# A trunk kernel's sample tile: V sums and gate products in two 64-column halves side by side, and identity products in TensorE's idle time

## What is computed

```python
h = h + mixer(rmsnorm(h, norm_mix))           # GLA and gated-delta heads, w_in, w_out
a = rmsnorm(h, norm_ffn)
q = a @ w_pq                                   # 8 heads, 2 halves of 128
idx, gate = top16_of_products(q, sub_keys)     # 16 experts of 16384 per token and head
hid = gelu(einsum('td,thkd->thk', a, u_tab[idx]))
h = h + einsum('thk,thkd->td', gate * hid, v_tab[idx])
gate = sigmoid(rmsnorm(h, norm_ple) @ w_ple_gate + b_ple_gate)
h = h + gate * (p @ w_ple_proj)
# after the last layer: y = rmsnorm(h, norm_final)
```

## Time and profile before

| | |
|---|---|
| median of three runs | 2375.65 us |
| profiled execution | 2375.78 us, span 2374.3 us |
| TensorE products | busy 1774.1 us, 75% |
| TensorE weight loads | busy 976.9 us, 41% |
| VectorE | busy 1452.3 us, 61% |
| ScalarE | busy 690.6 us, 29% |
| GpSimd | busy 1305.5 us, 55% |
| HBM read | 752.7 MB, 321 GB/s over the span |
| TensorE's granted clock, mean of the span | 0.874 of full speed |

### The profile page before, as it was taken

The page is one execution under the profiler, slowest core; times in us unless marked ns, Lnnn a source line. Parts: engine busy times, 40 slices in busy tenths (PEclk is TensorE's granted clock), DMA queues, the critical chain, the costliest instruction groups (busy, mean ns, idle before and its releaser), DMA issues.

```text
span 2374.3 us, 26318 instructions
## 1 busy us (share of the span) xinstructions
PE 1774.1 (75%) x9032; PEld 976.9 (41%) x9032; DVE 1452.3 (61%) x3698; ACT 690.6 (29%) x1641; POOL 1305.5 (55%) x1387
## 2 busy tenths in 40 slices
PE   7999998766566655579889999977655566555897
PEld 5768763322122211135567687533221222112354
DVE  2545556666766766676426446656666777667665
ACT  3323332222223222232333323322221332322232
POOL 2022257667777777767300232566677777776762
PEclk9999998888768778799999999988887777687999
DMA  8320299999999999999663204999999999999994
GB/s 242 107 91 22 84 394 400 406 406 406 409 409 409 409 409 409 409 405 404 232 204 108 81 15 149 393 402 406 406 406 409 409 409 409 409 409 406 407 402 161
DMA packets 268450, 763.26 MB, mean 321 GB/s; under 512 B 27002, under 2 KB 99634, under 8 KB 268312
## 3 DMA queue, kind: packets, MB, share of 16 engines
q0 software_dynamic: 187424, 682.78, 72.8%
q1 hardware_dynamic: 80888, 78.74, 10.4%
HBM read 752.70 MB, written 8.72 MB: 321 GB/s over the span
## 4 chain that ended last, share of the span: by engine, by line
PE 36%; DMA 32%; POOL 14%; DVE 9%; issue 6%; ACT 3%; SPq 0%; DVEq 0%; POOLq 0%; ACTq 0%
PE ps L1922 35%; DMA arena<-in_peer_u_dram,idx_u 32%; POOL arena L776 8%; POOL arena L785 6%; DVE arena L1439 3%; ACT arena L1103 1%; DVE arena L1628 0%; DVE arena L1326 0%; PE ps L1930 0%; DMA h<-in_x_sample_dram 0%; DVE wgt L1447 0%; DVE xn L1831 0%; ACT L853 0%; DVE top L1276 0%; ACT xn L1070 0%
## 5 line engine op out<-in xcount | busy, mean ns | idle before, releaser
L1922 PE MATMUL ps<-arena 64*64 64x512 f32 (+6 forms) x5856 | 1063.1, 668 | 540.9 <-ACT arena L1103 529.0
L1439 DVE CUSTOM_DVE_ANT_0 arena<-arena,ps 128x1024 f32<-128x1024 f32 x640 | 779.9, 1221 | 516.2 <-DMA arena<-in_peer_u_dram,idx_u 492.7
L1922 PEld LDWEIGHTS ps<-arena 64*64 64x64 f32 (+4 forms) x5856 | 444.6, 180 | 1098.9 <-issue 968.7
L785 POOL DMA_INDIRECT arena<-in_peer_v_dram,idx_u x640 | 605.0, 945 | 304.7 <-PE ps L1922 166.7
L776 POOL DMA_INDIRECT arena<-in_peer_u_dram,idx_u x640 | 609.3, 952 | 247.2 <-issue 173.7
L1922 PE MATMUL ps<-aT,wring 128*128 128x320 f32 (+1 forms) x1280 | 368.2, 444 | 2.3 <-ACT aT L1079 2.3
L1096 ACT ACTIVATE gelu<-hid 128x4 f32<-128x4 f32 x160 | 32.9, 206 | 1079.2 <-DVE hid L1439 1079.2
L1922 PEld LDWEIGHTS ps<-aT,wring 128*128 128x128 f32 x1280 | 244.2, 196 | 146.4 <-issue 58.2
L1922 PE MATMUL ps<-wring,aT 128*128 128x256 f32 x960 | 219.2, 383 | 3.1 <-DVE h L1810 1.6
L1922 PEld LDWEIGHTS ps<-wring,aT 128*128 128x128 f32 x960 | 179.1, 190 | 49.0 <-issue 26.9
L1103 ACT ACTIVATE arena<-ident,wgt 128x128 f32<-128x128 f32 x512 | 163.5, 390 | 72.9 <-DVE wgt L1447 72.9
(11 more groups left out here) (338 smaller groups left out, 1343.2 us busy)
## 6 DMA issues: line engine op xcount, KB each, us to landing
wring<-in_w_in_dram SPq DMA_DIRECT2D x28, 1024.0 KB, 5.6
wring<-in_w_peer_q_dram SPq DMA_DIRECT2D x18, 1024.0 KB, 18.3
arena<-in_peer_u_dram,idx_u POOLq DMA_INDIRECT x640, 16.2
arena<-in_peer_v_dram,idx_u POOLq DMA_INDIRECT x640, 15.9
wring<-in_w_out_dram SPq DMA_DIRECT2D x8, 1024.0 KB, 5.1
wring<-in_w_ple_gate_dram SPq DMA_DIRECT2D x8, 1024.0 KB, 16.6
arena<-in_state_gdn_dram POOLq DMA_DIRECT2D x2, 2048.0 KB, 18.9
out_dram<-arena SPq DMA_DIRECT2D x2, 2048.0 KB, 8.7
```

The source lines that it names most:

```text
L785: pool.indirect_dma_start(vrow[:, n % G, :], None, v_l, bass.IndirectOffsetOnAxis(ap=at, axis=0)).then_inc(v_loaded[n % G], 16)
L1439: dve.tensor_tensor_reduce(out=urow[:, n % G, :], in0=urow[:, n % G, :], in1=x_bank, scale=1.0, scalar=0.0, op0=ALU.mult, op1=ALU.add, acc ...
L1922: return pe.matmul(out, lhsT, rhs, start=start, stop=stop, skip_group_check=True)
```

## The change

For tile 2, whose doubled half is given up in most places:

- TensorE's V products: the stationary is 128 x 64 (ScalarE writes 64 columns of diag), bank m of the sum goes to partitions 64m to 64m+63, so the two products of an expert stand on the two column halves of the array. A first pair with the identity puts h itself into the sum. The sum is then copied into h, bank 0 by VectorE (64 rows), bank 1 by ScalarE (copy_half, from the upper partitions to the lower).
- The gates: for each r in 0, 1 the products m = 2r and 2r+1 alternate over k, 64 columns each, into the lower and the upper half. VectorE's work after them goes by r (2 times) and not by m (4 times). project does the same with its outputs; next_scale, square, the transposes and the last scaling work on 64 rows.
- GpSimd copies h's sample rows to the upper partitions at the start of each layer, which the mixer's w_out sum and the experts still need; VectorE and GpSimd wait for it (gvm_ready 1; the old gvm_ready 1 becomes 2).
- v1 of tile 2 is made by two 64-column products side by side, so that it still lies in both halves; aT is copied without its last 64 columns.
- keep_busy(n) issues n products of the identity with reset (320 columns) into bank 7, which nobody reads: 5 before the first layer, 6 before the last quad (with a wait for ple_done 8 ahead), 14 after the gates.

The diff, cut to its core:

```diff
@@ -305,11 +305,13 @@
-            return ps[:, 4 + m if i == 2 else 6 + m % 2, 0:WCOLS]
+            if i == 2:
+                return ps[HALF * (m % 2):HALF * (m % 2) + HALF, 4 + m // 2, 0:WCOLS]
+            return ps[:, 6 + m % 2, 0:WCOLS]
-                return ps[:, 2 + m // 2, WCOLS * (m % 2):WCOLS * (m % 2 + 1)]
+                return ps[HALF * (m % 2):HALF * (m % 2) + HALF, 2 + m // 2, 0:WCOLS]
...
@@ -668,6 +671,8 @@
+                pool.wait_ge(start_norm, 9)
+                pool.tensor_copy(h[HALF:P, 2, :], h[0:HALF, 2, :]).then_inc(gvm_ready, 1)
...
@@ -675,6 +680,7 @@
+                pool.wait_ge(gvm_ready, 1)
...
@@ -827,7 +833,7 @@
-                    act.activation(aT[:, k, :], ps[:, k % 4, 0:TILES * P], ACT.Copy,
+                    act.activation(aT[:, k, 0:NT], ps[:, k % 4, 0:NT], ACT.Copy,
...
@@ -1098,9 +1104,10 @@
+                    cols = P if step < 2 * HP else HALF
-                        act.activation(diag[:, n % G, :], unit[:, :], ACT.Copy,
+                        act.activation(diag[:, n % G, 0:cols], unit[:, 0:cols], ACT.Copy,
...
@@ -1144,9 +1151,18 @@
-                    act.wait_ge(h_added, i + 1 if i < 2 else 4)
-                    act.activation(xn[:, i, :], h[:, i, :], ACT.Square,
-                                   accum_out=ssq[:, i:i + 1]).then_inc(sq_done, 1)
+                    R = ROWS[i]
+                    act.wait_ge(h_added, i + 1)
+                    if i == 2:
+                        act.wait_ge(h_copied, 1)
+                    act.activation(xn[0:R, i, :], h[0:R, i, :], ACT.Square,
+                                   accum_out=ssq[0:R, i:i + 1]).then_inc(sq_done, 1)
+                def copy_half():
+                    act.wait_ge(v_free, G + TOPK * NSTEP)
+                    act.activation(h[0:HALF, 2, BANK:2 * BANK], ps[HALF:P, ACC_BANK[2] + 1, :],
+                                   ACT.Copy).then_inc(h_copied, 1)
...
@@ -1204,16 +1221,16 @@
+                copy_half()
-                for m in range(4):
-                    act.wait_ge(ple_biased, m + 1)
-                    act.activation(sig[:, m % 2, :], sig[:, m % 2, :], ACT.Sigmoid
-                                   ).then_inc(ple_sig, 1)
+                for r in range(2):
+                    act.wait_ge(ple_biased, r + 1)
+                    act.activation(sig[:, r, :], sig[:, r, :], ACT.Sigmoid).then_inc(ple_sig, 1)
-                act.activation(rstd[:, 2:3], ssq[:, 2:3], ACT.Sqrt).then_inc(std_ready, 1)
+                act.activation(rstd[0:HALF, 2:3], ssq[0:HALF, 2:3], ACT.Sqrt).then_inc(std_ready, 1)
...
@@ -1457,14 +1474,16 @@
-                    for b in range(2):
-                        c = slice(BANK * b, BANK * (b + 1))
-                        dve.tensor_tensor(h[:, i, c], h[:, i, c], bank(ACC_BANK[i] + b), ALU.add
-                                          ).then_inc(h_added, 1)
+                    dve.tensor_copy(h[0:HALF, i, 0:BANK], ps[0:HALF, ACC_BANK[i], :]
+                                    ).then_inc(h_added, 1)
-                dve.tensor_scalar(ssq[:, i:i + 1], ssq[:, i:i + 1], 1.0 / D, EPS, ALU.mult,
+                if i == 2:
+                    dve.tensor_scalar(ssq[HALF:P, i:i + 1], ssq[0:HALF, i:i + 1], 1.0 / D, EPS,
+                                      ALU.mult, ALU.add)
+                R = ROWS[i]
+                dve.tensor_scalar(ssq[0:R, i:i + 1], ssq[0:R, i:i + 1], 1.0 / D, EPS, ALU.mult,
...
@@ -1776,6 +1797,7 @@
+                dve.wait_ge(gvm_ready, 1)
...
@@ -1891,21 +1913,32 @@
-                for m in range(4):
-                    c = slice(WCOLS * m, WCOLS * (m + 1))
-                    dve.wait_ge(ple_mm, 9 + m)
-                    dve.scalar_tensor_tensor(sig[:, m % 2, :], gate_of(2, m), rstd[:, 2:3],
-                                             gain_row[:, c], ALU.mult, ALU.add
-                                             ).then_inc(ple_biased, 1)
-                    embed(2, m, own)
-                    dve.wait_ge(ple_done, 9 + m)
+                for r in range(2):
+                    dve.wait_ge(ple_mm, 9 + r)
+                    for g_ in range(2):
+                        rows, m = slice(HALF * g_, HALF * g_ + HALF), 2 * r + g_
+                        ins = dve.scalar_tensor_tensor(
+                            sig[rows, r, :], gate_of(2, m), rstd[rows, 2:3],
+                            gain_row[rows, WCOLS * m:WCOLS * (m + 1)], ALU.mult, ALU.add)
+                    ins.then_inc(ple_biased, 1)
+                    dve.wait_ge(ple_sig, 9 + r)
+                    own.after(dve.tensor_tensor(sig[:, r, :], sig[:, r, :], ps[:, 2 + r, 0:WCOLS],
+                                                ALU.mult))
+                    own.settle()
+                    for g_ in range(2):
+                        there = h[0:HALF, 2, WCOLS * (2 * r + g_):WCOLS * (2 * r + g_ + 1)]
+                        own.after(dve.tensor_tensor(
+                            there, there, sig[HALF * g_:HALF * g_ + HALF, r, :], ALU.add))
+                    own.settle()
+                    c = slice(BANK * r, BANK * (r + 1))
-                        out=xn[:, 2, c], in0=h[:, 2, c], in1=h[:, 2, c], scale=1.0, scalar=0.0,
-                        op0=ALU.mult, op1=ALU.add, accum_out=ssq_part[:, m:m + 1]))
+                        out=xn[0:HALF, 2, c], in0=h[0:HALF, 2, c], in1=h[0:HALF, 2, c], scale=1.0,
+                        scalar=0.0, op0=ALU.mult, op1=ALU.add, accum_out=ssq_part[0:HALF, r:r + 1]))
-                own.after(dve.tensor_reduce(ssq[:, 2:3], ssq_part[:, :], AX, ALU.add))
+                own.after(dve.tensor_tensor(ssq[0:HALF, 2:3], ssq_part[0:HALF, 0:1],
+                                            ssq_part[0:HALF, 1:2], ALU.add))
-                dve.tensor_scalar(ssq[:, 2:3], ssq[:, 2:3], 1.0 / D, EPS, ALU.mult, ALU.add
+                dve.tensor_scalar(ssq[0:HALF, 2:3], ssq[0:HALF, 2:3], 1.0 / D, EPS, ALU.mult, ALU.add
...
@@ -1913,7 +1946,9 @@
-                dve.tensor_tensor(xn[:, i, :], xn[:, i, :], fin_row, ALU.mult).then_inc(xn_ready, 1)
+                R = ROWS[i]
+                dve.tensor_tensor(xn[0:R, i, :], xn[0:R, i, :], fin_row[0:R, :], ALU.mult
+                                  ).then_inc(xn_ready, 1)
...
@@ -1958,7 +1993,13 @@
+            def keep_busy(count):
+                for _ in range(count):
+                    mm(ps[:, 7, 0:NT], ident[:, :], reset[:, :])
+            keep_busy(5)
...
@@ -1999,8 +2040,10 @@
-                            ins = mm(ps[:, b, 0:WCOLS], aT[:, k, P * i:P * (i + 1)],
-                                     wring[:, blk % RING, k, :], k == 0, k == KD - 1)
+                            for t0 in (0, HALF) if i == 2 else (0,):
+                                R = ROWS[i]
+                                ins = mm(ps[t0:t0 + R, b, 0:WCOLS], aT[:, k, COL[i]:COL[i] + R],
+                                         wring[:, blk % RING, k, :], k == 0, k == KD - 1)
...
@@ -2120,7 +2163,7 @@
-                pe.wait_ge(gvm_ready, 1)
+                pe.wait_ge(gvm_ready, 2)
...
@@ -2314,8 +2357,12 @@
-                                ins = mm(bank(ACC_BANK[tile] + m), diag[:, n % G, :],
-                                         vrow[:, n % G, BANK * m:BANK * (m + 1)], opens, False)
+                                there = ps[HALF * m:HALF * m + HALF, ACC_BANK[tile] + m, :]
+                                if opens:
+                                    mm(there, ident[0:HALF, 0:HALF],
+                                       h[0:HALF, 2, BANK * m:BANK * (m + 1)], True, False)
+                                ins = mm(there, diag[:, n % G, 0:HALF],
+                                         vrow[:, n % G, BANK * m:BANK * (m + 1)], False, False)
...
@@ -2462,7 +2509,7 @@
-                        mm(emb_of(i, m), pT[:, k, P * i:P * (i + 1)],
+                        mm(emb_of(i, m), pT[:, k, COL[i]:COL[i] + ROWS[i]],
...
@@ -2491,6 +2538,9 @@
+                    if q4 == NQUAD - 1:
+                        pe.wait_ge(ple_done, 8)
+                        keep_busy(6)
...
@@ -2508,21 +2558,27 @@
-                    pe.wait_ge(h_added, 3 + b)
+                    if b == 0:
+                        pe.wait_ge(h_added, 3)
+                    else:
+                        pe.wait_ge(h_copied, 1)
-                        ins = pe.transpose(heads(TURN_BANK[2] + b)[:, k % 4, :],
-                                           h[:, 2, P * k:P * (k + 1)], ident[:, :])
+                        ins = pe.transpose(heads(TURN_BANK[2] + b)[:, k % 4, 0:HALF],
+                                           h[0:HALF, 2, P * k:P * (k + 1)],
+                                           ident[0:HALF, 0:HALF])
-                for m in range(4):
+                for r in range(2):
-                        if m == 0 and k == 4:
+                        if r == 0 and k == 4:
-                        ins = mm(gate_of(2, m), aT[:, k, P * 2:P * 3],
```

(5 more changed lines are left out.)

16 lines of the change are left out of this document (10 added, 6 removed).

## The result

The changed kernel's median is 2374.52 us (20 runs, 2365.27 to 2388.21), the kernel before measured 2376.26 us beside it (20 runs, 2374.84 to 2394.65). The ratio is 0.9971 with a 95% interval of 0.9957 to 0.9984: 0.3% faster, where 15 us or 0.6% were forecast. Both kernels spread upwards, so the medians lie closer (1.7 us) than the means (5.4 us: 2372.99 and 2378.34). The time lies outside the range of 2354 to 2369. The profiled execution is one of the shorter ones: 2367.25 us, span 2365.7. The fastest executions of the two kernels lie 9.6 us apart (2365.27 and 2374.84), so the best runs gained more than the average ones.

The account below looks back on a forecast made before the run. TensorE products (35%) and landing u rows (32%) lead the waits: gathers bound expert stages, a serial chain each layer's tail. 2 x (6.6 tail + 0.9 stage) = 15.0 us off the 2375.65 median gave 2360.6 us; range 2354 to 2369.

Parts of the forecast that it names:

- The tail: End of each layer: shorter last quad and gates, with the fillers setting the end; 6.6 us less a layer.
- Rival A: Tail: the clock falls between last quad and gates, costing the gates 3.4 us a layer; 2367.4 us, chance 0.14.
- B: Column halves don't overlap in gates, last quad and v1 units: 21.6 us slower, 2397 us, chance 0.06.
- C: Weight loads of paired halves lie bare, 0.2 us more a pair, gates 13.4 us; 2374 us, chance 0.05.
- D: Layer's end: filler or meeting is cheaper, or the warm clock pays in layer 1; 2355.6 us, chance 0.09.
- The expert stage: Tile 2's gathers: 404 GB/s could become 409, 0 to 1.8 us less, taken as 0.9 us a layer.
- One pair, 0.9 us, hidden: Tile 2's expert stage: the product opening the sum with h is one pair, 0.9 us, hidden under the gathers.
- The v1 units: Tile 2's v1 products become pairs: same time, 0 to 0.2 us a unit, two units a layer.
- The opening: Before layer 0: five fillers hidden or repaid by transposes at full clock; taken as 0, bounds -1 to +2 us.

Follow-up runs that it names:

- e2: The changed kernel without the 14 filler products behind the gates: 2367.45 us, ratio 0.9959 to the kernel before.
- e6: The changed kernel with tile 2's two opening products issued early and 8 fillers behind the gates instead of 14: 2364.60 us, ratio 0.9938 to the kernel before.
- e1: The changed kernel run again without an edit: 2368.74 us, ratio 0.9966 to the kernel before.
- e12: The changed kernel with tile 2's v1 products issued for the lower 64 rows only, leaving part of the result wrong: 2374.92 us.
- e5: The changed kernel with tile 2's two opening products issued together ahead of the first diagonal: 2370.88 us, ratio 0.9960 to the kernel before.
- light pair: The changed kernel and the kernel before, both with most 16-column products in each mixer left out: 2342.58 and 2354.12 us.
- e10: The changed kernel with tile 2's gate products issued one column block after the other instead of alternating: 2376.42 us, ratio 0.9988 to the kernel before.

## Why the prediction was wrong

The tails came as forecast. What failed is the stage's 1.8 us (a rate read as time), the changes of tile in the v1 units (put at nothing), and the time of the mixers, which the sum took as fixed.

- **The tail: right.** Forecast for the gates' records 7.0 us, measured 7.13; last quad 3.7, measured 4.00 and 3.92; gates' start 7.3 us behind the weights, measured 7.04; VectorE's end 19.4, measured 19.4; fillers 7.8, measured 7.80, ending at 22.1, measured 21.9; gain 6.6 a layer, measured 6.9 to 7.0. The fillers set the end, as said (e2, e6).
- **Rival A came partly true.** In 8 of the 22 tails of kernels whose gates alternate the gates take 8.8 us, in the rest 7.1, and in all eight the granted clock falls at their start (0.57 in e1's first 4 us). That is 8 x 1.7 / 22 = 0.6 us a layer in the mean. I had set it as all or nothing at 3.4 us.
- **Rivals B and C are out.** Pairs run side by side on shared rows (7.13 us), and e12 shows a second product for nothing. D is out too, since the layer's end comes 2.4 us earlier with eight fillers or none.
- **The expert stage, 0.9 us a layer: wrong.** The failing step is "404 GB/s could become 409", read as time. e5 restored the rate of the two windows and not a tenth of the time: the chain waits for u rows, and the slack that TensorE got there had no taker. From the first to the last weights of tile 2 it takes 154.9 to 155.1 us in the changed kernel's profiles and 154.5 to 154.9 in those of before, 0.3 us longer and not 0.9 shorter. "One pair, 0.9 us, hidden" was wrong in the first part (three products one by one, 5.4 us until the second diagonal could start) and right in the second.
- **The v1 units, "same time, 0 to 0.2 us a unit": mis-sized.** 0.69 us a layer for two units, at the changes between whole and half columns, and the long stretch got nothing back from the narrower copies of aT.
- **The opening: right in its outcome.** 5 fillers at 1.2 GHz, transposes at 2.4, no change at the long stretch's start (33.44, 33.39 before). The sum for the low clock was slightly off: 12.75 + 2 x 2.8 is 18.3 and not 18.1.
- **The mixers: not in the prediction at all.** I took work that the change doesn't touch as fixed and put it at nothing without a reason. It holds the two pieces that vary most. By the profiles the changed family pays 2.7 us a layer more there, 5.5 us a kernel; since the profiles of before are favourable, that is the upper end. By the profiles it is the largest term that the sum lacked. The clock is shown as what moves it; why the changed kernel meets more low clock there stays open.

The sum with measured terms, mixers apart: -13.8 (tails) + 1.4 (v1) + 0.6 (stage) + 1.2 (gates) = -10.6 us. The timed means lie 5.4 (the result), 8.4 (e1) and 9.0 us (e5) under before's, which leaves 1.6 to 5.2 us a kernel for the mixers, where the profiles say 5.5. In the light pair, where P280 doesn't vary and no gates were slow, the difference is 11.5 to 11.7 us, near -13.8 + 1.4 + 0.6 = -11.8. So against the forecast of 15.0 us, which had 1.8 from the stage, the losses are 2.4 us (stage), 1.4 (v1), 1.2 (gates) and 1.6 to 5.5 (mixers), and the tails gave 0.6 more than forecast.

## What to carry to other kernels

Before you turn GB/s into time, ask whose rows are missing: where two streams share the engines of the DMA, look at the rate of the stream on the chain. Two products on different halves of the columns, on all 128 rows, cost what one costs if they stand next to each other in the queue; alternate them, and don't mix in another tile shape. And when a kernel runs in long dense stretches at a clock that falls, take several profiles of before, and compare their own times with the mean of the timed runs before you count anything in them: a change that is worth 0.5% can lose a good part of it in code that it doesn't touch, and a few lucky profiles of before make that part look larger.

## What the runs showed of the hardware

- The clock falls without any break in the work: TensorE busy 10.00 of 10 us while groups of 16-column and 128-column products alternate, granted 0.64 to 0.67 (e1). With most of the 16-column products gone P280 took 25.18 us in four layers of four.
- At the launch's start the five fillers run at 0.53 us a record, half rate, while the window shows a granted clock of 1.00:

```profile
15.00:18.00 3.00, 3.00 (x9) 1.87 (x8) 0.98 (x2) 0.00 (x0) 1.03 (x1) 1.00 1.07 365
```

  Before the first stretch of work the duration of a known product tells the clock, the view doesn't.
- Products of 64 x 64 and 128 x 64 that alternate run one by one, even where neighbours stand on different column halves: they start 1.6 to 1.9 us apart at a granted clock near 0.5 (the changed kernel, 1007 to 1012). The pair of 64 x 64 products next to each other takes 1.04 us at 1.00 (e5), so by estimate 2.1 us at the low clock for both.
- A record of 256 columns costs 0.22 us on whole columns and as much on half of them, and 0.11 when the halves alternate (7.13 / 64). Issued block after block the two halves still overlap at each border, by four records (e10).
- A change between whole and half columns costs 0.17 us (0.69 us for four in the v1 group, e12 and the changed kernel).
